# The first pieces of a decoder layer on one core: x piece 0 on ScalarE's queue, its high part on VectorE, norm weights carried in x's rows, three k tiles by terms

## The reference

```python
x = x + 0.5 * swiglu_ffn(x, ffn1_norm, ffn1_w_gate, ffn1_w_up, ffn1_w_down)
h = rms_norm(x, mix_norm)
# gated DeltaNet (4 heads x 128), block-sparse attention (4 x 64), attention into 256 memory tokens (4 x 64)
y = concatenate([y_gdn, y_moba, y_mem])        # all from h @ w_in, the last also from rms_norm(mem)
x = x + y @ w_out
x = x + 0.5 * swiglu_ffn(x, ffn2_norm, ffn2_w_gate, ffn2_w_up, ffn2_w_down)

def swiglu_ffn(x, gain, w_gate, w_up, w_down):
    h = rms_norm(x, gain)
    return (silu(h @ w_gate) * (h @ w_up)) @ w_down
```

## Time and profile before

| | us |
|---|---|
| median of 3 runs | 994.4 |
| lowest and highest | 994.15, 994.59 |
| the profiled execution | 994.35 |
| its span in the trace | 992.5 |
| PE busy | 987.5 |
| DVE busy | 685.7 |
| ACT busy | 444.7 |
| POOL busy | 509.7 |

### The profile page before, as it was taken

The page is one execution under the profiler, slowest core; times in us unless marked ns, Lnnn a source line. Parts: engine busy times, 40 slices in busy tenths (PEclk is TensorE's granted clock), DMA queues, the critical chain, the costliest instruction groups (busy, mean ns, idle before and its releaser), DMA issues.

```text
span 992.5 us, 16521 instructions
## 1 busy us (share of the span) xinstructions
PE 987.5 (99%) x6833; PEld 872.2 (88%) x6833; DVE 685.7 (69%) x1092; ACT 444.7 (45%) x655; POOL 509.7 (51%) x297
## 2 busy tenths in 40 slices
PE   9999999999999999999999999999999999999998
PEld 7888999999999988788877888888999999999997
DVE  6894976676666497863547764789986676666745
ACT  8642444344443472534456764634343334433341
POOL 0355775676656433543252301645975666756741
PEclk9999999999999999999999999999999999999999
DMA  8432322332123312321221001322132333123312
GB/s 312 154 130 79 128 86 86 128 128 97 74 86 127 114 57 86 127 86 43 85 87 44 3 2 44 127 85 86 50 122 85 128 128 118 53 86 127 128 43 85
DMA packets 15914, 95.33 MB, mean 96 GB/s; under 512 B 2016, under 2 KB 2400, under 8 KB 5600
## 3 DMA queue, kind: packets, MB, share of 16 engines
q1 hardware_dynamic: 15696, 94.23, 26.4%
q10 hardware_dynamic: 144, 0.05, 0.0%
HBM read 92.17 MB, written 2.10 MB: 95 GB/s over the span
## 4 chain that ended last, share of the span: by engine, by line
PE 96%; DVE 3%; POOL 1%; issue 0%; ACT 0%; DVEq 0%; POOLq 0%
PE bank L2016 50%; PE bank L2142 35%; PE bank L2456 1%; PE bank L2542 1%; PE bank L2460 1%; PE bank L2482 1%; PE bank L2570 1%; PE bank L2559 1%; PE bank L2504 1%; PE bank L2194 1%; POOL wlo L517 0%; PE bank L2526 0%; DVE t_ffn_sum L1339 0%; PE bank L2606 0%; PE bank L2516 0%; PE bank L2628 0%
## 5 line engine op out<-in xcount | busy, mean ns | idle before, releaser
L2142 PE MATMUL bank<-t_ffn_hi,whi 128*128 128x256 f32 x952 | 269.4, 283 | 0.0
L2142 PE MATMUL bank<-t_ffn_hi,wlo 128*128 128x256 f32 x952 | 269.4, 283 | 0.0
L2142 PE MATMUL bank<-t_ffn_lo,whi 128*128 128x256 f32 x952 | 269.4, 283 | 0.0
L534 POOL TENSOR_TENSOR wlo<-sums,whi 128x512 fp32r<-128x512 f32 x136 | 184.7, 1380 | 131.8 <-ACT whi L739 131.7
L517 POOL TENSOR_TENSOR wlo<-raw,whi 128x1024 fp32r<-128x1024 f32 (+1 forms) x36 | 124.6, 3478 | 166.2 <-ACT whi L614 151.3
L534 POOL TENSOR_TENSOR wlo<-raw,whi 128x512 fp32r<-128x512 f32 x102 | 168.4, 1665 | 41.0 <-ACT whi L739 41.0
L2142 PEld LDWEIGHTS bank<-t_ffn_hi,whi 128*128 128x128 f32 x952 | 182.7, 192 | 0.7
L2142 PEld LDWEIGHTS bank<-t_ffn_lo,whi 128*128 128x128 f32 x952 | 182.7, 192 | 0.7
L2142 PEld LDWEIGHTS bank<-t_ffn_hi,wlo 128*128 128x128 f32 x952 | 182.7, 192 | 0.0
L2016 PE MATMUL bank<-ahi,whi 128*128 128x512 f32 x396 | 156.5, 395 | 0.4 <-POOL wlo L517 0.4
L2016 PE MATMUL bank<-ahi,wlo 128*128 128x512 f32 x396 | 154.4, 390 | 0.0
(11 more groups left out here) (339 smaller groups left out, 1405.1 us busy)
## 6 DMA issues: line engine op xcount, KB each, us to landing
raw<-fast_in SPq DMA_DIRECT2D x34, 1024.0 KB, 4.9
raw<-stream SPq DMA_DIRECT2D x26, 1024.0 KB, 4.9
raw_down<-fast_in SPq DMA_DIRECT2D x19, 1024.0 KB, 7.0
raw<-stream SPq DMA_DIRECT2D x7, 512.0 KB, 7.9
out<-x SPq DMA_DIRECT2D x7, 256.0 KB, 2.0
x<-x_in SPq DMA_DIRECT2D x3, 512.0 KB, 8.7
memx<-mem_in SPq DMA_DIRECT2D x2, 512.0 KB, 11.1
raw_gate<-stream SPq DMA_DIRECT2D x1, 1024.0 KB, 5.0
```

The lines of the kernel that those rows point to most:

```text
L534: nc.gpsimd.tensor_tensor(in_ring(wlo, ring_at, n), whole[:, PIECE * at:PIECE * (at + 1)], in_ring(whi, ring_at, n).bitcast(F32), ALU.subt ...
L2142: ins = E.matmul(psum[bank][:, HALF * h:HALF * (h + 1)], a, b[:, k, :], start=start and k == 0 and m == 0, stop=k == K2 - 1 and m == 2, sk ...
```

## The change

What it does:

- The eight norm weights of the first norm are put ahead of x in each partition's row, in HBM and in SBUF: the new tile `xg` is 128 x (8 + 8 x 512), and `x` is a view of it. `small` has eight columns less. `col` reads a negative column number from `xg`.
- x0, with those eight columns, is issued by ScalarE in the place where it issued `small`. SP issues w0, w1, x1, w2, x2 and so on, and `small` after x4.
- ahi 0 is made by VectorE, as its first instruction, ahead of wlo 0. ScalarE makes the other seven and waits ahead of the first of them for ahi 0.
- The waits for `small_sem` move behind all of x's parts, on both engines.
- `first_pair` goes term by term for k = 0, 1 and 2, with a wait ahead of each term (high parts; low part of the weights; low part of x), and bank by bank from k = 3.
- `warm` has 128 columns, read four times over by each warm-up matmul; there are ten of them in place of eleven.

The core of the diff:

```diff
-        x, _, _ = place("x", [P, KD, T])
+        xg, _, _ = place("xg", [P, KD + KD * T])
+        x = xg[:, KD:KD + KD * T].rearrange("p (k t) -> p k t", k=KD)
...
-            return small[:, c:c + 1]
+            return small[:, c:c + 1] if c >= 0 else xg[:, KD + c:KD + c + 1]
...
-                sp.dma_start(x[:, k0:k1, :], x_in[:, k0:k1, :]).then_inc(x_sem[i], 16)
+                x0, x1 = KD + k0 * T if k0 else 0, KD + k1 * T
+                if i > 0:
+                    sp.dma_start(xg[:, x0:x1], x_in[:, x0:x1]).then_inc(x_sem[i], 16)
+            sp.dma_start(small[:], small_in).then_inc(small_sem, 16)
...
-            A.dma_start(small[:], small_in).then_inc(small_sem, 16)
-
+            A.dma_start(xg[:, 0:KD + T], x_in[:, 0:KD + T]).then_inc(x_sem[0], 16)
...
-                if i == 0:
-                    act.wait_ge(small_sem, 16)
                 act.wait_ge(x_sem[i], 16)
-                for d in range(PIECES[i], PIECES[i + 1]):
+                for d in range(max(PIECES[i], 1), PIECES[i + 1]):
+                    if d == 1:
+                        act.wait_ge(a_hi, 1)
                     x_high(0, S_G1, d)
...
+            dve.wait_ge(x_sem[0], 16)
+            V.tensor_scalar(x_hi[0][:, 0, :], x[:, 0, :], col(S_G1), None, ALU.mult).then_inc(a_hi, 1)
             for i in range(NP):
...
-                pe.wait_ge(piece_hi, 1)
-                pe.wait_ge(a_hi, 1)
-                for (w, act_), (done, count) in zip(((whi, ahi), (wlo, ahi), (whi, alo)),
-                                                    ((a_hi, 1), (piece_lo, 1), (a_lo, 1))):
-                    pe.wait_ge(done, count)
-                    for bank in range(4):
-                        E.matmul(psum[bank][:], wslice(w, 0, 0, bank * P, P, PAIR), act_[:, 0, :],
-                                 start=w is whi and act_ is ahi, stop=False)
-                for k in range(1, KD):
+                for k in range(3):
+                    low = (piece_lo, k + 1) if k < 2 else (w_lo, 1)
+                    pe.wait_ge(*((piece_hi, k + 1) if k < 2 else (w_hi, 1)))
+                    for (w, act_), (done, count) in zip(((whi, ahi), (wlo, ahi), (whi, alo)),
+                                                        ((a_hi, k + 1), low, (a_lo, k + 1))):
+                        pe.wait_ge(done, count)
+                        for bank in range(4):
+                            E.matmul(psum[bank][:], wslice(w, 0, k, bank * P, P, PAIR), act_[:, k, :],
+                                     start=k == 0 and w is whi and act_ is ahi, stop=False)
+                for k in range(3, KD):
...
-                    for _ in range(11):
-                        E.matmul(psum[4][:], warm[:, 0:P], warm[:], start=True, stop=True)
+                    for _ in range(10):
+                        E.matmul(heads(4), warm[:], warm[:].unsqueeze(1).broadcast_to([P, H, P]), start=True, stop=True)
```

More of the change, by code:

```diff
@@ L64 @@
 C_N = C_PICK + 12
-S_G1, S_GM, S_G2, S_GMEM = 0, KD, 2 * KD, 3 * KD
-S_CONV = 4 * KD
+S_G1, S_GM, S_G2, S_GMEM = -KD, 0, KD, 2 * KD
+S_CONV = 3 * KD
 S_OG = S_CONV + 12 * 4
@@ L187, in build @@
         memsq, _, _ = place("memsq", [P, KD, M], at=cq_at)
-        warm, _, _ = place("warm", [P, T], F32R, at=mid)
+        warm, _, _ = place("warm", [P, P], F32R, at=mid)
         msum, _, _ = place("msum", [P, M], at=at_at + 3 * M * 4)
@@ L661, in _ @@
                 x_square(0, d)
+            act.wait_ge(small_sem, 16)
             A.activation(gain_qk[:, 0:1], col(S_MQ), ACT.Copy, scale=col(S_MK)).then_inc(gain_ready, 1)
@@ L1238, in _ @@
                     part_lo(u, c0, c1, piece_hi, n + 1, piece_lo)
-                if i == 0:
-                    dve.wait_ge(small_sem, 16)
                 for d in range(PIECES[i], PIECES[i + 1]):
                     x_low(0, S_G1, d)
+            dve.wait_ge(small_sem, 16)
             dve.wait_ge(gain_ready, 2)
@@ L2945 @@
     small = np.concatenate(
-        [per_partition(a[n][0]) for n in ("ffn1_norm", "mix_norm", "ffn2_norm", "mem_norm")]
+        [per_partition(a[n][0]) for n in ("mix_norm", "ffn2_norm", "mem_norm")]
         + [a["gdn_conv_w"][0].reshape(4, 12, P).transpose(2, 1, 0).reshape(P, 48), a["gdn_out_norm"][0][:, None]]
@@ L2954 @@
         "fast_in": np.stack(fast),
-        "x_in": a["x"][0].T.reshape(KD, P, T).transpose(1, 0, 2),
+        "x_in": np.concatenate([per_partition(a["ffn1_norm"][0]),
+                                a["x"][0].T.reshape(KD, P, T).transpose(1, 0, 2).reshape(P, KD * T)], axis=1),
         "mem_in": a["mem"][0].T.reshape(KD, P, M).transpose(1, 0, 2),
```

## The result

| | before | changed |
|---|---|---|
| median, us | 994.41 | 998.30 |
| lowest and highest | 994.15, 994.59 | 998.19, 998.82 |
| runs | 6 | 6 |
| the profiled execution, and its span | 994.35, 992.5 | 998.55, 996.8 |

The ratio is 1.0041 (95% interval 1.0029 to 1.0052): slower by 3.9 us, where 0.4 less was forecast. The forecast gain is in the trace all the same, and something ten times its size is laid on top.

What follows compares the result with a forecast made beforehand. TensorE, busy 987.5 of 992.5 us, was taken as the bound, so only its start could gain: 994.4 less 0.31 (clock unmoved) or 0.5 (clock moved by the warm-up) gave 994.0 us, range 993.1 to 994.9.

Steps and rivals of the forecast that it cites:

- the part on k = 3 and after: From k = 3 on: order unchanged, no PE gap, the 0.31 us shift kept; x's 32-byte move costed at nothing, 0.1 either way.
- this sign: Whole span: if it changes by more than what k = 3 shows, the prediction is wrong and the difference comes from elsewhere.
- The steps of the opening: Warm-up, first operands, k = 0 to 2: PE starts at 5.90, k = 2 at 11.89 against 12.20, gaining 0.31 us.
- the upper bound of 6.16: PE's first real matmul: its start if w0 and x0 land at 5.38, against 5.90 expected.
- Two signs: VectorE's ahi 0 starts by 5.2; the x_sums pair of the statistic stands 0.3 us earlier than 35.48.
- the shift is carried on: From k = 3 to the end: the start's 0.31 us gain persists as long as nobody else is late.
- its rise as fixed to 6.87 or to the first matmul: Start: clock rises at 6.87, gain 0.31 us, or 0.33 sooner with the warm-up, at 6.55, gain about 0.5.
- The rivals: Other outcomes: clock or pieces earlier 0.2, nothing gained 0.1, x0 late 0.15, clock later 0.05.
- x0 did not land late: Rival at the start: x0 lands as late as 7.05, k = 2 0.94 us later, 995.3 us; chance 0.15.
- put off the rise: Rival at the start: PE's idling from 5.41 to 5.90 restarts the low clock level, 996.4 us; chance 0.05.
- no wait behind the start took the gain: Rival of no effect: a wait later in the kernel takes the shift back, 994.2 to 994.6 us; chance 0.1.
- Slower by over 0.2%: Whole kernel: a loss of about 2 us, which only the later clock reaches; chance 0.05.

Runs made afterwards that it cites:

- e1_aligned: Changed kernel with xg begun 32 bytes lower, so tiles lie at the byte offsets of the kernel before; 993.98 us, ratio 0.9993 to the kernel before.
- e2_shift32: Kernel before with 32 unused bytes ahead of x, while hhi, hlo, z, kt and the rest stay; 998.98 us, ratio 1.0044.
- e6_no_terms: e1_aligned with first_pair as in the kernel before, without the order by terms; 994.16 us in one execution.
- e7_old_warm: e1_aligned with the old warm-up of 128x512 zeros and eleven matmuls; 993.53 us in one execution.
- e9_map: Separate kernel outside the layer: groups of 24 matmuls, moving operand's distance from the weights varied; 512 columns took 0.2267 us at distance 0, 0.2333 at 32.
- e13_map2: The group kernel of e9_map with both operands moved, all 64 pairs of places; 512 columns took 0.227 us wherever the two begin together.
- e4_all32: Kernel before with every tile of the arena 32 bytes higher, so operand distances stay; 994.52 us, ratio 1.0000.

## Why the prediction was wrong

**The step that failed** is the last sentence of the part on k = 3 and after: x moves 32 bytes, "I find no row for that, and take nothing, with 0.1 us either way". It was priced by what lies at the moved tile, x, which TensorE never reads, and not by all that is placed behind it. The rows that carried the term were there, 354 hhi matmuls for each of three products; what they would cost in another place was not in the trace, and it measured 4.3 us (e1_aligned against the changed kernel) and 4.5 (e2_shift32 against before). The main terms, from the chains of the two kernels: the 306 cost 70.17 - 69.36 = 0.81, the 133 cost 31.05 - 30.23 = 0.82, the down blocks 0.29 for every 48, of which there are 15 between 125 and 940 us, 4.35; the full 256-column stretches give back 0.12 to 0.20 each. Taken along the kernel, the changed one is 0.38 ahead at k = 2 and 0.16 at 35.8, then 0.65 behind at 105, 2.0 at the end of the first FFN (372.6 against 370.6), still 2.1 at 600, 3.3 behind the 133 of the second FFN and 4.3 at the end. The prediction had named this sign: a span that changes by more than the start of k = 3 shows has its difference from elsewhere.

**The steps of the opening** nearly all came out. The warm-up started at 0.99 (0.98). w0 landed by 5.17 and x0 at 5.40 (5.1 for both; bound 5.38), ahi 0 took 0.49, TensorE started at 6.05 (5.90; the upper bound of 6.16 is 6.18 by the rows it is added up from), k = 1 at 9.10 (9.16), k = 2 at 11.82 (11.89) with no gap between: 0.38 us in place of 0.31. Two signs were missed: ahi 0 started at 5.42, not by 5.2, and the statistic stood 0.17 earlier, not 0.3, which is the placement again. That 0.38 came so near 0.31 is partly luck. Over all the traces taken k = 2 starts between 12.00 and 12.69 in the eight without the change and between 11.62 and 11.82 in the four with the whole of it, 0.6 us apart in the mean, since landings and the clock's rise differ from run to run. e6_no_terms bears out that without the order by terms nearly nothing would be left. x0 gained nothing by a queue of its own: it landed at 5.40 there and at 5.38 behind w0.

**Carried to the end.** "PE has no gap, so the shift is carried on" was true and no use: without gaps every nanosecond of a matmul is on the path. The three pairs with and without the change, at the same placement, differ by 0.5, 0.6 and 0.9 us (993.98 and 994.51, 987.42 and 988.05, 990.06 and 990.94), each near or inside its uncertainty, all of one sign.

**The clock.** I took its rise as fixed to 6.87 or to the first matmul. e7_old_warm, with a rise by 4.36 after a start at the same 1.31, rules out both. The Trainium skill, TensorE: Matmul & The Clock Gate, section "Part 1: The HAM clock gate", has the window run freely; by that rule the rise varies, and the runs agree (eleven equal warm-up matmuls took 5.06, 4.33 and 4.12 us). I gave the rule too little weight because whole executions differed by only 0.44.

**The rivals.** None was what happened. x0 did not land late; TensorE's pause from 5.6 to 6.05 did not put off the rise (spacings of 0.23 from 6.56 on, from 6.87 before); no wait behind the start took the gain. Slower by over 0.2% had 0.05, and that for the clock alone. No rival had the form "every matmul changes its pace".

## What to carry to other kernels

When a change alters the size of one tile, list every tile whose start moves, and check the distance of each matmul's two operands, counted round 256 bytes, before and after: a placement is part of the code of a kernel that TensorE bounds. Here equal starts were best for 512 columns, and with a distance of 96 bytes the slowest for 256. If the trace shows a new pace in stretches whose code is untouched, undo the offsets first: it is an edit of a few lines and settles it.

## What the runs showed of the hardware

- Float32r matmuls, each with new 128x128 weights, stand 0.2267 us apart for 512 columns when both operands begin at the same place round 256 bytes, 0.2292 at a distance of 64 bytes and 0.233 to 0.234 at all other multiples of 32 (e9_map, e13_map2). The layer agrees within 0.001 at 0, -32, -64, -96 and -128, and in the memory tokens' products at 32 and 64. For 256 columns it is 0.1196 at 0 and 96, 0.1179 at 32 and 64, 0.1138 or 0.118 at -64. It needs no other engine at work (the maps), and moving both operands together changes nothing in the layer (e4_all32: 994.52 against 994.51).
- The Trainium skill, TensorE: Matmul & The Clock Gate, section "Wait — 56ns, not 53.3ns?", has back-to-back matmuls of 512 columns 215.7 ns apart at the high level. No float32r stretch here, with new weights for each, came to that: the nearest is 226.7.
- At a distance of -64 the same 256-column matmuls run at one of two paces, 0.1138 or 0.118 (e13_map2: L118 and L128), and can go over from one to the other within a group (L146). Why, and why the distance counts at all (which part of reading weights and moving data meets the other), no run tells.
- The clock's rise moved by some 3 us between runs whose warm-up starts at the same 1.31 (first short spacing from 4.36 in e7_old_warm, from 7.39 in e2_shift32). Each matmul of 512 columns that runs at the low level on the path costs 0.2 us (0.427 against 0.227).
